# Scores of two query blocks in one visit, and one strip tile for two heads, in a two-layer hybrid attention kernel

## The chip, the cores and the metric

The kernel runs on one core of one Trainium2 chip. The metric is the device time of one execution in microseconds, here the median of three. A core has five engines that run their own streams of instructions side by side and wait for each other through semaphores: TensorE (matmuls and transposes; PE in the profile, PEld for the loads of its stationary operand), VectorE (DVE), ScalarE (ACT), GpSimd (POOL) and SyncE (SP), which here issues most DMAs. TensorE writes to eight banks of PSUM; everything else stands in SBUF.

## The reference

Two identical layers over 1,040 tokens (16 meta tokens ahead of 1,024 drawn ones) with 1,024 features, all in float32. A layer projects x with one matrix and feeds four mixers of eight heads with 64 features each; every mixer's output is multiplied by a SiLU gate, and one output projection, a scaled residual and a layer norm end the layer. Each mixer computes

```
logits = q @ k.T * scale (+ bias or decay), masked by position
probs  = softmax(logits)
out    = probs @ v
```

- A (forgetting attention): dense causal attention, the logits get a decay, cumsum(log f)[t] - cumsum(log f)[s].
- B (latent attention): q and k come from small latents; 32 rotary features are added to the 64 plain ones, so the logits are a sum of two products.
- C (sparse attention): an indexer scores all keys, and each query attends only to its 256 best.
- D (sliding window of 128 keys, with a learned sink in the softmax's sum).

## The kernel before, in words

**Tiles.** The tokens form nine blocks, 0 to 8: block 0 holds the 16 meta tokens, the others 128 tokens each. In A, B and C a query block i of 128 rows attends to 128 i + 16 keys. Keys are cut at multiples of 128 of the packed order, so i tiles of 128 keys are followed by a tile of 16, the "strip". In D a block attends to at most 256 keys in two tiles. The eight heads of a mixer are worked in four pairs, p = 0 to 3, and the two heads of a pair are e = 0 and 1.

**The order of work.** A class `Plan` writes one list of items, and each engine walks through it and issues its part of each item; the list thus sets the order on each engine. A layer runs the branches in the order A, D, B, C, then the output projection and the layer norm. In the first layer (profile times) A runs from 242 to 541 us, D to 797, B to 1080 and C to 1325. `pair` (L366) writes the items of one pair: it goes through the query blocks in `ORDER`, 8 down to 0 (L31), one step each. In the second layer block 0's queries aren't needed, and `empty_step` (L464) takes the step's place. A step of block i writes:

- `qk`: TensorE multiplies q of the block by the keys (L1100; in B a second product with the 32 rotary features, L1111). The scores of both heads go to score banks; a product has up to 512 columns, and `score_products` (L84) cuts it. VectorE adds the bias or mask, takes each row's maximum and writes the scores to a row of `probs` (L1565). `probs` has three rows of different length (`ROW_AT`), used in turn. In A and C, GpSimd prepares the mask of the diagonal first (`tri` L1637, `near` L1652).
- `rec` (of the step before, `normalise` L508): VectorE takes the reciprocal of the sums (L1576, L1577) and GpSimd multiplies the row by it (L1664), once a head.
- `pv` (`values` L493): if the transposes of an odd block were written in the step before, TensorE multiplies the transposed probabilities of the two blocks 2a - 1 and 2a by v (L1136), all into the bank O_BANK. `pv_parts` (L147) lists its products: 2a - 1 tiles with both blocks' 256 query columns, one with 128 columns, and two strips with 16 key rows and 32 columns each. The product is written for e = 0 and 1.
- `tp` for e = 0, then 1, of the block two steps back (`LAG` = 2; `probabilities` L481): TensorE transposes its tiles (L1123) in groups of up to four (`t_groups` L119) into one of two banks of `ps_t`, and ScalarE or VectorE copies each group to the buffer X or Y of `arena` (L1298). Block 8 has nine tiles a head and so three groups. A strip is a transpose like the others, of 16 columns to 16 rows.
- `exp` (L1287): ScalarE's exponential with its sum, one for each head. `gt` (L1585): VectorE multiplies pv's result by the gate. `top`: a number of steps of the top-256 search for branch C (L1328, L1330), set for each step by `TOP_RATE`.
- filler: projections (`tile`, `q_latent`, `k_latent`, `token_block`) for the gate and for the next pair or branch. Each chunk of 340 to 348 columns (L1057, in B L1066) goes through one bank, `P_BANK`, which ScalarE or VectorE empties: the gate by ScalarE (L1255) and then VectorE (L1503), B's rotary chunks by VectorE (L1516 to L1521). The next chunk waits for that.

`flush` (L513) writes what is still pending after the last pair of a branch.

**Waits.** A `pv` waits until all its groups have been copied (`all_left`, L725). A transpose group waits until its bank of `ps_t` has been emptied (`bank_left`, L732). A score product waits until VectorE has read what stood in its banks before. VectorE waits, before it writes a row of `probs`, for the transposes that read the row's last content (`rwaits`).

Most of TensorE's stream in these branches is L1057, L1066, L1100, L1111, L1123 and L1136. A float32 matmul is run as two passes, and the profile counts each pass as an instruction.

## Time and profile before

| | before |
|---|---|
| median of three runs | 3070.66 us (3069.75 to 3072.55) |
| the profiled execution: its time | 3073.53 us |
| its span | 3071.7 us |
| TensorE busy, matmuls | 2929.9 us, 95% |
| VectorE busy | 1656.8 us, 54% |
| ScalarE busy | 1032.8 us, 34% |
| GpSimd busy | 549.7 us, 18% |
| mean granted clock of TensorE over the span | 0.992 |

The span is the time from the profile's first instruction to its last. Times in the rows are microseconds from its start. The granted clock is a share of TensorE's full 2.4 GHz, and 0.50 is its lower level. In a timeline, operations of one form that follow each other are one line: start, duration, engine, line of the code, operation, output and inputs with partitions x elements (for TensorE stationary and moving operand), the number of instructions, and in brackets the idle time before it and what ended it. An end of a matmul is modelled, so its duration is less exact than the start of the next line.

### The profile page before, as it was taken

Reading aid. Unit: us, or ns where it says so; the run is one execution under the profiler, and the core shown is the slowest. Engines: PE = TensorE matmul, PEld = TensorE weight load, DVE = VectorE, ACT = ScalarE, POOL = GpSimd, SP = SyncE. Lnnn points to the kernel's source line nnn. Section 1 sums busy time; section 2 is a strip of 40 time slices with the busy share of each in tenths; the row PEclk is TensorE's granted clock in tenths of the full one; section 3 lists DMA queues with packets and bytes.
Section 4 is the critical chain, followed back from the end, with each engine's and each line's share of the span. In section 5 each row is a group of like instructions: output and inputs, shape, how many; then the busy total and the mean of one; then the engine's idle time right before and its main releaser. Section 6 shows DMA issues by size and latency. Waiting matters only on the chain. (4 is left out here: it accounts for less than half of the span.)

```text
span 3071.7 us, 40390 instructions
## 1 busy us (share of the span) xinstructions
PE 2929.9 (95%) x14262; PEld 1702.8 (55%) x14262; DVE 1656.8 (54%) x4445; ACT 1032.8 (34%) x3121; POOL 549.7 (18%) x946
## 2 busy tenths in 40 slices
PE   7999999998899999999999999999988999999998
PEld 5446666555466666644544466665554666665443
DVE  5338877766777433312233388777667764323222
ACT  3233333333444344410012333333334443444000
POOL 1002222111122133300000022221111111334000
PEclk9999999999999999999999999999999999999999
DMA  5101111101000021042120011111010001210421
GB/s 213 58 14 39 42 43 32 44 27 45 22 17 18 20 79 54 25 143 82 55 87 29 14 39 42 42 32 44 27 51 15 17 18 32 95 32 25 154 82 41
DMA packets 89102, 152.69 MB, mean 50 GB/s; under 512 B 10640, under 2 KB 66592, under 8 KB 86856
## 3 DMA queue, kind: packets, MB, share of 16 engines
q1 hardware_dynamic: 88904, 150.12, 14.9%
q8 instruction: 116, 1.90, 0.3%
q14 instruction: 82, 0.67, 0.1%
HBM read 120.12 MB, written 32.08 MB: 50 GB/s over the span
## 5 line engine op out<-in xcount | busy, mean ns | idle before, releaser
L1057 PE MATMUL ps_s<-xT,w_ring 128*128 128x348 f32 (+4 forms) x3616 | 1127.8, 466 | 11.9 <-DVE arena L1407 4.8
L1057 PEld LDWEIGHTS ps_s<-xT,w_ring 128*128 128x128 f32 x3616 | 674.3, 191 | 407.3 <-issue 113.2
L1664 POOL TENSOR_SCALAR arena<-arena,small 128x1040 f32<-128x1040 f32 (+8 forms) x544 | 353.3, 661 | 1450.6 <-DVE small L1577 1449.3
L1298 ACT ACTIVATE arena<-ps_t 16x32 f32<-16x32 f32 (+4 forms) x1096 | 331.2, 357 | 306.0 <-PE ps_t L1123 298.6
L1287 ACT ACTIVATE arena<-arena,small 128x1040 f32<-128x1040 f32 (+8 forms) x544 | 369.0, 678 | 149.9 <-DVE small L1565 149.7
L1328 DVE MAX8 small<-score 128x8 f32<-128x1040 f32 (+6 forms) x448 | 376.3, 840 | 10.5
L1330 DVE MATCH_REPLACE8 score<-small,score 128x1040 f32<-128x1040 f32 (+6 forms) x448 | 370.0, 826 | 0.0
L1123 PE MATMUL ps_t<-ident,arena 128*128 128x128 f32 (+2 forms) x2400 | 347.3, 277 | 23.0 <-ACT arena L1298 22.0
L1123 PEld LDWEIGHTS ps_t<-ident,arena 128*128 128x128 f32 (+2 forms) x2400 | 252.4, 132 | 149.7 <-issue 78.3
L1136 PE MATMUL ps_o<-arena 128*64 128x256 f32 (+3 forms) x3136 | 282.2, 320 | 19.6 <-ACT arena L1298 18.1
L1100 PE MATMUL ps_s<-feat 64*128 64x272 f32 (+12 forms) x1680 | 296.0, 455 | 3.0 <-ACT squares L1213 3.0
L1151 PE MATMUL ps_s<-arena,feat 128*128 128x512 f32 x640 | 284.8, 597 | 3.5 <-DMA feat<-mixed 3.5
L1136 PEld LDWEIGHTS ps_o<-arena 128*64 128x64 f32 (+1 forms) x3136 | 184.4, 135 | 154.1 <-issue 48.8
L1151 PEld LDWEIGHTS ps_s<-arena,feat 128*128 128x128 f32 x640 | 121.8, 192 | 154.1 <-issue 149.0
L1100 PEld LDWEIGHTS ps_s<-feat 64*128 64x128 f32 (+1 forms) x1680 | 136.6, 183 | 92.3 <-issue 73.2
L1492 DVE SCALAR_TENSOR_TENSOR score<-arena,small,score 128x1040 f32<-128x1040 f32 (+6 forms) x98 | 87.8, 901 | 153.9 <-ACT arena L1272 148.1
L1027 PE MATMUL ps_s<-arena,xT 128*128 128x144 f32 (+1 forms) x512 | 149.7, 446 | 1.6 <-ACT cT L1231 1.6
L1255 ACT ACTIVATE gate<-ps_s 128x348 f32<-128x348 f32 (+3 forms) x96 | 44.0, 458 | 279.7 <-PE ps_s L1057 279.7
L1585 DVE SCALAR_TENSOR_TENSOR mixg<-ps_o,gate 128x256 f32<-128x256 f32 (+1 forms) x144 | 56.3, 391 | 140.1 <-PE ps_o L1136 139.7
L1503 DVE SCALAR_TENSOR_TENSOR gate<-gate,ps_s 128x348 f32<-128x348 f32 (+3 forms) x96 | 48.9, 510 | 145.9 <-ACT gate L1255 145.6
L1027 PE MATMUL ps_s<-vw,xT 128*128 128x512 f32 x256 | 114.0, 598 | 3.0 <-ACT squares L1213 3.0
L1027 PEld LDWEIGHTS ps_s<-arena,xT 128*128 128x128 f32 x512 | 81.2, 194 | 62.0 <-issue 61.9
(161 smaller groups left out, 2229.6 us busy)
## 6 DMA issues: line engine op xcount, KB each, us to landing
w_ring<-in_w_feat SPq DMA_DIRECT2D x78, 512.0 KB, 3.5
mixed<-mixg SPq DMA_DIRECT2D x128, 128.0 KB, 1.7
feat<-mixed SPq DMA_DIRECT2D x16, 1024.0 KB, 6.7
resid<-score SPq DMA_DIRECT2D x16, 512.0 KB, 3.1
score<-resid SPq DMA_DIRECT2D x16, 512.0 KB, 7.6
arena<-in_w_out SPq DMA_DIRECT2D x4, 1536.0 KB, 9.0
cT<-falls SPq DMA_DIRECT2D x8, 520.0 KB, 4.8
feat<-falls SPq DMA_DIRECT2D x8, 520.0 KB, 5.3
```

Source lines behind the costliest of these rows:

```text
L1027: mm = pe.matmul(ps_s[0:M, bank, 0:n], xT[:, k, cols], wv[:, k, :], start=(k == 0), stop=(k == KT - 1))
L1057: mm = pe.matmul(ps_s[:, bank, 0:w], w_ring[:, wt % 2, k, :], xT[:, k, c0:c0 + w], start=(k == 0), stop=(k == KT - 1))
L1100: mm = pe.matmul(score_bank(ch, e)[0:M, 0:ch["w"]], q[r:r + HD, qc], k[r:r + HD, k0 + ch["c0"]:k0 + ch["c0"] + ch["w"]], start=True, stop= ...
L1123: mm = pe.transpose(ps_t[0:w, tg % 2, c * BLK:c * BLK + M], p_row(it, h, k0, w), ident[0:M, 0:M])
L1136: mm = pe.matmul(ps_o[HD * e:HD * e + HD, at:at + w], v_of(br, p, e, kb, rows), arena[0:rows, src:src + w], start=(j == 0), stop=(j == len ...
L1151: mm = pe.matmul(ps_s[0:M, bank, :], mix_in[slot][:, k, 0:M], w_out[k][:, cols], start=(k == 0), stop=(k == 15))
L1287: nc.scalar.activation(p, p, ACT.Exp, scale=-1.0, bias=nm[:, e:e + 1], accum_out=psums[0:M, st % 4, e:e + 1]).then_inc(S["exp_done"], 1)
L1298: a = nc.scalar.activation(dst, src, ACT.Copy)
L1328: dve.max(top8, sc).then_inc(S["top_step"], 1)
L1330: dve.match_replace(sc, top8, sc, TAKEN).then_inc(S["top_step"], 1)
L1492: dve.scalar_tensor_tensor(sc, src, w, sc, ALU.mult, ALU.add).then_inc(S["acc_done"], 1)
L1664: nc.gpsimd.tensor_scalar(p, p, rinv[0:M, st % 4, e:e + 1], 1.0, ALU.mult, ALU.mult).then_inc(S["nrm_done"], 1)
```

## The change

**Rounds.** `rounds_of` lists which query blocks' scores are issued in one `qk` item: in D 8 and 7, 6 and 5, 4 and 3, 2 and 1, and 0 alone; in A, B and C 8 to 4 alone, then 3 and 2, then 1 and 0 (without 0 in the second layer, and `empty_step` follows the last round). One `qk` item has both blocks' score products behind each other on TensorE, in B first all products of 64 features and then all of 32, and both blocks' maxima behind each other on VectorE. Then comes `rec` for the blocks of the round before (in D it comes ahead of `qk`), and `values` once; then, for each of the two blocks, the rest of the step as before, with the lag of two steps. `row_of` gives new places in `probs`, so that two blocks can stand in one row. In B, block 3 (400 keys) is one score product and no longer two, and so is block 2 (272 keys).

**Strips.** GpSimd normalises the 16 strip columns of each head not in place but into a new tile `strips` (128 x 4 x 48, the heads at columns 0 and 32) with an instruction of its own, ahead of the one for the rest. One transpose of 48 columns then serves both heads, in the last group of e = 1. `t_groups` cuts the groups accordingly: block 8 has two groups for e = 0 (before: three), block 4 one (before: two). In the buffers X and Y the strips of a head stand in a 256-column area at the end (`strips_at`), the odd block's from column 96. `pv_parts` has one product fewer: the odd block's strip and the tile beside it are one product of 160 columns with 128 rows, and the even strip has 128 rows too. The rows beyond 16 are zeros, written by GpSimd (`strip_zero`) in A's first pair of each layer; v's rows beyond block 8's 16 are zeroed at the start.

**The wait of pv.** A `pv` waits first for all groups but the last, and ahead of the first product that reads the last group's tiles for that one (`last_from`); where there is a single group it waits for it at its start.

**Size.** The program sets a dynamic DMA scratch size of 8,192.

The core of the diff ("..." where lines are left out):

```diff
+STRIP_ODD = BLK - 32
 P_BANK, O_BANK, T_BANK = 4, 5, 6
+STRIPS = 2
...
+def rounds_of(br):
+    return [[8, 7], [6, 5], [4, 3], [2, 1], [0]] if br == "D" else [[8], [7], [6], [5], [4], [3, 2], [1, 0]]
+def row_of(br, i):
+    if br == "D":
+        n = NB - 1 - i
+        return (0, 256 * n) if n < 4 else (1, 256 * (n - 4)) if n < 6 else (2, 256 * (n - 6))
+    return {3: (2, 0), 2: (2, keys_of(3)), 1: (1, 0), 0: (2, keys_of(3) + keys_of(2))}.get(i, ((NB - 1 - i) % 3, 0))
...
-        products = even(n, 2 if n >= 272 else 1)
+        products = even(n, 2 if i > 3 else 1)
...
-    if br == "D" or i <= 1:
+    if br == "D" or i == 0:
         return [both([kb for kb in range(max(i - 1, 0), i + 1)])] if e else []
-    parts = -(-(i + 1) // 4)
-    size = -(-(i + 1) // parts)
-    return [[(e, kb) for kb in range(c, min(c + size, i + 1))] for c in range(0, i + 1, size)]
+    if i == 1:
+        return [both([0]) + [(STRIPS, i)]] if e else []
+    tiles = [(e, kb) for kb in range(i)] + ([(STRIPS, i)] if e else [])
+    parts = -(-len(tiles) // 4)
+    size = -(-len(tiles) // parts)
+    return [tiles[c:c + size] for c in range(0, len(tiles), size)]
+def tile_at(a, kb):
+    return PT_HEAD[buffer_of(a)] + 256 * (kb - 2 * a)
+def strips_at(a):
+    return PT_HEAD[buffer_of(a)] - 256
...
+    a = (i + 1) // 2
     if kb == i:
-        return 256 * i + 32 if i % 2 else 256 * (i - 1)
-    return kb * 256 + (0 if i % 2 else BLK)
+        return strips_at(a) + (STRIP_ODD if i % 2 else 0)
+    return tile_at(a, kb) + (0 if i % 2 else BLK)
...
-    at = 256 * (2 * a - 1)
-    return ([(kb, BLK, 256 * kb, 256, 0) for kb in range(2 * a - 1)] + [(2 * a - 1, BLK, at + BLK, BLK, BLK),
-            (2 * a - 1, N_META, at + 32, 32, 96), (2 * a, N_META, at, 32, 224)])
+    at = strips_at(a)
+    return ([(kb, BLK, tile_at(a, kb), 256, 0) for kb in range(2 * a - 1)]
+            + [(2 * a - 1, BLK, at + STRIP_ODD, 256 - STRIP_ODD, STRIP_ODD), (2 * a, BLK, at, 32, 224)])
...
+        for blocks in rounds_of(br):
+            if l == DEPTH - 1 and 0 in blocks:
+                blocks = blocks[:-1]
+            steps = [self.step(l, br, p, i, hu) for i in blocks]
+            if br == "D":
+                self.normalise()
+            for s in steps:
+                if br == "A":
+                    self.add("tri", **s)
+                if br == "C":
+                    self.add("near", **s)
+            if steps:
+                self.add("qk", l=l, br=br, p=p, idx=steps[0]["idx"], hu=hu, steps=steps)
+                self.normalise()
+                self.values()
+            self.pending += steps
+            for s in steps:
+                if early and s["idx"] == NB - 1:
+                    early()
+                old = self.pending.pop(0) if len(self.pending) > LAG else None
+                if old and old["i"] == 0:
+                    self.values()
+                self.probabilities(old, 0)
+                self.add("exp", e=0, **s)
+                self.gated()
+                self.add("top", l=l, count=TOP_RATE[br][s["idx"]])
+                work = fill.get(s["idx"], [])
+                for fn in work[:1]:
+                    fn()
+                self.probabilities(old, 1)
+                self.add("exp", e=1, **s)
+                for fn in work[1:]:
+                    fn()
+            self.rec_next += steps
+        if l == DEPTH - 1:
+            self.empty_step(l, br, early, fill.get(NB - 1, []))
...
+        row, at = row_of(br, i)
...
-                self.pv_next = dict(s, need=tg + len(groups))
+                own = [kb for h, kb in groups[-1] if h != STRIPS] if len(groups) > 1 else [0]
+                self.pv_next = dict(s, need=tg + len(groups), last_from=own[0])
...
+            for c, (h, kb) in enumerate(group):
+                if h == STRIPS:
+                    m0, m1 = c * BLK + it["M"] - asks(it["br"], it["i"], kb), c * BLK + it["M"]
+                    for e in range(2):
+                        at = pt_at(it["buf"], e) + pt_col(it["br"], it["i"], kb)
+                        out.append((arena[0:N_META, at:at + m1 - m0], ps_t[32 * e:32 * e + N_META, tg % 2, m0:m1]))
...
+                    for s in it["steps"]:
+                        i, M = s["i"], s["M"]
+                        k0 = keys_of(i) - s["n"]
+                        for ch in s["products"]:
+                            waits(pe, ch["waits"])
...
-                        for j, ch in enumerate(it["products"]):
+                        for j, (s, ch) in enumerate((s, ch) for s in it["steps"] for ch in s["products"]):
+                            i, M = s["i"], s["M"]
                             for e in range(2):
                                 r = HD * (j % 2) + ROPE * e
-                                pe.matmul(score_bank(ch, e)[0:M, 0:ch["w"]], qr[r:r + ROPE, qc],
+                                pe.matmul(score_bank(ch, e)[0:M, 0:ch["w"]], qr[r:r + ROPE, tok0(i):tok0(i) + M],
...
+                            if h == STRIPS:
+                                mm = pe.transpose(ps_t[0:3 * N_META, tg % 2, c * BLK:c * BLK + M],
+                                                  strips[0:M, it["strip"], :], ident[0:M, 0:M])
+                                continue
...
-                    all_left(pe, it["need"])
+                    if it["last_from"]:
+                        all_left(pe, it["need"] - 1)
...
+                        if j == it["last_from"]:
+                            all_left(pe, it["need"])
...
-                    waits(dve, it["rwaits"])
...
+                    for s in it["steps"]:
+                        waits(dve, s["rwaits"])
+                        maxima(s)
...
-            link(nc.gpsimd.memset(fz[:], 0.0))
+            link(nc.gpsimd.memset(v_tok[:, NB - 1, :], 0.0))
+            link(nc.gpsimd.memset(cv_tok[:, NB - 1, :], 0.0))
+            link(nc.gpsimd.memset(strips[:], 0.0))
...
+                    if it["idx"] == 0 and p == 0:
+                        pool.wait_ge(S["pj_full"], vw_used[(l, "TA")])
+                        for buf in "XY":
+                            z = strip_rows(buf)
+                            nc.gpsimd.memset(z, 0.0).then_inc(S["strip_zero"], 1)
...
-                        p = p_row(it, e, 0, it["n"])
-                        nc.gpsimd.tensor_scalar(p, p, rinv[0:M, st % 4, e:e + 1], 1.0, ALU.mult, ALU.mult
-                                                ).then_inc(S["nrm_done"], 1)
+                        inv = rinv[0:M, st % 4, e:e + 1]
+                        if it["br"] == "D" or it["i"] == 0:
+                            p = p_row(it, e, 0, it["n"])
+                            nc.gpsimd.tensor_scalar(p, p, inv, 1.0, ALU.mult, ALU.mult).then_inc(S["nrm_done"], 1)
+                            continue
+                        n = it["n"] - N_META
+                        nc.gpsimd.tensor_scalar(strips[0:M, it["strip"], 2 * N_META * e:2 * N_META * e + N_META],
+                                                p_row(it, e, n, N_META), inv, 1.0, ALU.mult, ALU.mult)
+                        p = p_row(it, e, 0, n)
+                        nc.gpsimd.tensor_scalar(p, p, inv, 1.0, ALU.mult, ALU.mult).then_inc(S["nrm_done"], 1)
...
-    nc = bacc.Bacc("TRN2", target_bir_lowering=False, num_devices=1)
+    nc = bacc.Bacc("TRN2", target_bir_lowering=False, num_devices=1, dynamic_dma_scratch_size=8192)
```

## Rows read from the trace of the kernel before

**Rows 1.** The page: busy time, share of the span and instructions of each engine.
```profile
PE 2929.9 (95%) x14262; PEld 1702.8 (55%) x14262; DVE 1656.8 (54%) x4445; ACT 1032.8 (34%) x3121; POOL 549.7 (18%) x946
```

**Rows 2.** Waits of TensorE: line, releaser: total us, times, longest.
```profile
PE ps_t L1123 <- ACT arena L1298: 22.0, 62, 0.6
PE ps_o L1136 <- ACT arena L1298: 18.1, 24, 1.4
```

**Rows 3.** Groups by shape: line, operation, xcount | busy, mean ns | idle.
```profile
L1123 PE MATMUL ps_t<-ident,arena 128*16 128x128 f32 x400 | 107.4, 273 | 0.0
...
L1664 POOL TENSOR_SCALAR arena<-arena,small 16x16 f32<-16x16 f32 x32 | 8.3, 268 | 81.4 <-DVE small L1577 81.4
```

**Rows 4.** Timeline of TensorE, branch A: start, us, operation xcount.
```profile
441.62 0.82 PE L1123 MATMUL ps_t<-ident,arena 128*128 128x128 f32 x6
442.37 0.73 PE L1100 MATMUL ps_s<-feat 64*128 64x272 f32 x4
443.08 2.95 PE L1136 MATMUL ps_o<-arena 128*64 128x256 f32 x32
445.96 0.76 PE L1123 MATMUL ps_t<-ident,arena 128*128 128x128 f32 x5
446.56 4.85 PE L1057 MATMUL ps_s<-xT,w_ring 128*128 128x348 f32 x16
451.24 0.71 PE L1123 MATMUL ps_t<-ident,arena 128*128 128x128 f32 x5
```

**Rows 5.** The same stretch, TensorE's weight loads (PEld).
```profile
445.61 0.31 PEld L1136 LDWEIGHTS ps_o<-arena 16*64 16x64 f32 x8 [0.17 <-issue]
```

**Rows 6.** Timeline of TensorE in branch D.
```profile
701.68 0.60 PE L1123 MATMUL ps_t<-ident,arena 128*128 128x128 f32 x4
702.21 0.70 PE L1100 MATMUL ps_s<-feat 64*128 64x256 f32 x4
703.03 1.09 PE L1136 MATMUL ps_o<-arena 128*64 128x256 f32 x12
```

**Rows 7.** Timeline of VectorE and TensorE in D, at a gate chunk.
```profile
547.02 0.51 DVE L1503 SCALAR_TENSOR_TENSOR gate<-gate,ps_s 128x344 f32<-128x344 f32 x1
...
548.70 0.56 PE L1057 MATMUL ps_s<-xT,w_ring 128*128 128x348 f32 x1
```

**Rows 8.** Timeline of TensorE in branch B, pair 1.
```profile
915.75 0.95 PE L1100 MATMUL ps_s<-feat 64*128 64x200 f32 x8
...
918.88 1.40 PE L1066 MATMUL ps_s<-cT,vw 128*128 128x344 f32 x4 [0.83 <-DVE feat L1521]
920.11 0.82 PE L1123 MATMUL ps_t<-ident,arena 128*128 128x128 f32 x6
920.86 0.73 PE L1100 MATMUL ps_s<-feat 64*128 64x136 f32 x8
...
921.97 2.95 PE L1136 MATMUL ps_o<-arena 128*64 128x256 f32 x32
...
925.45 1.39 PE L1066 MATMUL ps_s<-cT,vw 128*128 128x348 f32 x4
```

**Rows 9.** Timeline of VectorE in the same stretch.
```profile
924.95 0.33 DVE L1521 COPY feat<-feat 64x344 f32<-64x344 f32 x1
```

**Rows 10.** Timeline of TensorE in branch B, pair 0.
```profile
854.59 2.63 PE L1066 MATMUL ps_s<-cT,vw 128*128 128x344 f32 x4 [2.16 <-DVE feat L1521]
857.02 1.21 PE L1123 MATMUL ps_t<-ident,arena 128*128 128x128 f32 x6
858.16 0.73 PE L1100 MATMUL ps_s<-feat 64*128 64x136 f32 x8
```

**Rows 11.** Windows in B, pair 0: us, busy time by engine, PEclk, DMA share.
```profile
854.40:857.80 3.40, 3.21 (x8) 2.17 (x9) 3.30 (x15) 0.72 (x2) 1.61 (x2) 0.50 0.00 0
```

**Rows 12.** Timeline of TensorE in branch C.
```profile
1139.13 2.08 PE L1136 MATMUL ps_o<-arena 128*64 128x256 f32 x24 [0.97 <-ACT arena L1298]
...
1197.76 0.74 PE L1123 MATMUL ps_t<-ident,arena 128*128 128x128 f32 x5 [0.51 <-ACT arena L1298]
```

More of the change, by code:

```diff
@@ new lines, in pair, with step @@
+        if l == DEPTH - 1:
+            self.empty_step(l, br, early, fill.get(NB - 1, []))
+        return None
+    def step(self, l, br, p, i, hu):
+        st = self.take("st")
+        chunks, products = [], []
+        some = score_products(br, i)
+        for nth, ((c0, w), pieces) in enumerate(some):
+            banks = self.slot_for(len(some), nth, P_BANK)
+            last = self.n["chunk"] + len(pieces) - 1
+            waits = self.banks(banks, ("max_done", 2 * (last + 1)))
+            if O_BANK in banks:
+                waits = latest(waits + [("o_free", self.n["pv"])])
+            products.append(dict(c0=c0, w=w, banks=banks, pieces=len(pieces), waits=waits))
+            chunks += [dict(c0=a, w=b, banks=banks, at=a - c0, g=self.take("chunk"), full=2 * (last + 1))
+                       for a, b in pieces]
+        row, at = row_of(br, i)
+        owner = self.row_owner[row]
+        n = min(keys_of(i), 2 * BLK) if br == "D" else keys_of(i)
+        return dict(l=l, br=br, p=p, i=i, st=st, idx=NB - 1 - i, n=n, M=rows_of(i), chunks=chunks, products=products,
+                    row=row, at=ROW_AT[row] + at, strip=(NB - 1 - i) % 4,
+                    rwaits=latest([owner] if owner else []), a=(i + 1) // 2, hu=hu,
+                    ds=self.take("ds") if br == "D" else None, tri=self.take("tri") if br == "A" else None,
+                    nb=self.take("nb") if br == "C" else None)
@@ L766, in copies @@
             out = []
+            for c, (h, kb) in enumerate(group):
[4 more added lines that the diff above has]
+                        out.append((arena[0:N_META, at:at + m1 - m0], ps_t[32 * e:32 * e + N_META, tg % 2, m0:m1]))
+            if all(h == STRIPS for h, _ in group):
+                return out
             runs, per = copy_runs(it["br"], it["i"], group)
```

133 lines of the change are left out of this document (46 added, 87 removed).

## The prediction

> **What bounds the kernel now.** The page's engine table comes first [rows 1]: TensorE is busy 95% of the span, and with one core that makes every hole and every instruction on TensorE count directly. The waits of TensorE come second [rows 2]: the largest sum is 22.0 us in 62 pieces, transposes that wait until ScalarE has emptied a bank of ps_t, about 0.35 us each. So the end is set by TensorE's own order of work, and a gain must come from fewer or cheaper instructions there; a loss comes where the new order makes it wait for somebody. I then read stretches of its timeline, one in each branch, beside VectorE's.
>
> **The joined strip's transposes.** Six transposes stand between 441.62 and 442.37, four between 701.68 and 702.21 [rows 4, 6]; the difference of two is 0.22 us, so one is 0.11. Each query block i from 1 to 8 of branches A, B and C gives up one: the two heads' 16-column strips become one 48-column tile. That is 8 blocks x 3 branches x 4 pairs x 2 layers = 192 of the 400 narrow ones [rows 3], 192 x 0.11 = 21 us. The same moving columns pass through, so I price the joined one like a single one. The ScalarE copies stay as many.
>
> **The strip's products.** Every matmul of the program stands twice in the trace (two passes of f32). The sixteen-row products are 8 instructions at the end of a sum; their weight loads start at 445.61, behind 0.17 us of idle, and the next transposes start at 445.96 [rows 4, 5], so the strips cost 0.35 us after a change of array shape that costs about 0.09 more (four transposes need 0.44 and the row shows 0.53 before the scores of [rows 6]). In all 0.44. Afterwards the odd strip rides in the tile beside it, 160 columns instead of 128: 16 products of 348 columns run from 446.56 to 451.24, 4.68 us [rows 4], so a column costs 0.84 ns a pass, 32 more in two passes 0.05 us. The even strip stays as two passes, 0.06 each, with 128 rows, and the way out of the shape costs what it did, 0.09. 0.44 - 0.05 - 0.12 - 0.09 = 0.18 us for each of the 4 products a pair with a >= 1: 96 x 0.18 = 17 us.
>
> **Fewer groups.** Block 8 has 9 tiles of head 0 now, in three groups, and the third waits; with 8 it has two. 24 times about 0.3 [rows 2]: 7 us. Starting pv before its last group is copied I cost at nothing: only 24 products wait today, 18.1 us in all [rows 2], and they are those of D and of the small blocks, as blocks 4 and 3 in C at 1139.13 [rows 12], whose last transposes are a single group in the new plan too.
>
> **Joined rounds, on the gain side.** A visit to the scores of one 256-column block lasts 0.82 us (702.21 to 703.03) and its columns are 2 x 256 x 0.84 ns = 0.43 [rows 4, 6]; the rest, and 0.09 on the way in, is paid once for two blocks. 0.82 - 0.43 + 0.09 = 0.48 per joining in D, 4 a pair in either layer, 32 x 0.48 = 15.5 us. In A, B and C the block of 272 columns takes 442.37 to 443.08, 0.71, with 2 x 272 x 0.84 = 0.46 of columns [rows 4]: 0.25 + 0.09, of which 0.06 goes back because pv loses a neighbour of its own array shape in some places; 0.28. There are 24 joinings in layer 0 and 12 in layer 1 (block 0 is gone): 36 x 0.28 = 10, and 2 for the third shape that B enters once instead of twice. Sum 28 us; below, nothing (if a second block pays its loads again), above, 0.6 each (the whole visit but for its columns, and both changes of shape), 68 x 0.6 = 41.
>
> **Joined rounds, what they put in the way.** The second block's scores, and the product pv that used to follow, were also cover: while TensorE did them, VectorE and ScalarE emptied the one projection bank (P_BANK). Now both maxima passes stand on VectorE ahead of that eviction, and the cover stands later.
> - B, pairs 0 to 2, blocks 3 and 2. Before: scores of 3 at 915.75, third rotary chunk at 918.88 (it waited 0.83 for VectorE), scores of 2 at 920.86, pv at 921.97, next chunk at 925.45 [rows 8]. VectorE finished the rotary chunk's copy at 924.95 + 0.33 = 925.28, only 0.17 earlier [rows 9]: this stretch is already VectorE's. In the new order VectorE has block 2's maxima (0.75) ahead of it and 0.27 less for block 3, so the next chunk can start at 925.8; TensorE gets there at 920.11 + 0.65 for six transposes + 0.3 for the bank + 0.44 for four, 921.5, and waits 4.3 us, while the 2.9 us of pv and the scores come after. Pair 0 is alike, pair 2 has narrower top-k steps: 4.3, 4.3 and 3.5, 12 a layer, 24 us. What idleness does to the clock stands in [rows 10, 11]: after 2.16 us without work the granted clock was 0.50 (1.2 instead of 2.4 GHz) for 3.4 us, four chunks took 2.43 us (854.59 to 857.02) against 1.23 (918.88 to 920.11), the transposes behind them 1.14 against 0.75, 1.6 us in all. Six times: 9 us. B: 33 us; bounds 20 (waits of 2.5 and 5 of clock) and 50 (each wait 2 longer, the same clock twice in two places).
> - D. A gate chunk's eviction ended at 547.02 + 0.51 = 547.53, and the next projection began at 548.70 [rows 7]: 1.2 us of slack. A joined round brings 0.8 us more of maxima and 0.7 of sums that wait for the exponential ahead of it on VectorE, and TensorE arrives 0.6 to 1.8 sooner. Three of four pairs then wait 0.5 to 1.8: 12 us over both layers. In layer 0 the product pv of block 1 comes straight behind its transposes, without scores between: 4 x 1.0. The last D steps and the w_tb projections lose 0.6 of cover at about ten boundaries: 6. Together 22; bounds 5 and 35.
> - A. Blocks 5 and 4 now make three groups in a row, 8 x 0.35; the last K chunk is directly ahead of the next pair's scores, 8 x 0.15; in pair 0 VectorE is late, 2 x 0.6. 5 us. The long projection (4.7 us) hides the rest.
> - C has no projection in the last three steps. Waits like the 0.51 at 1197.76 [rows 12] move and grow to about 1.5 in front of blocks 1 and 0, while the 0.97 us that the product of blocks 4 and 3 waits at 1139.13 goes, since block 2's transposes now stand ahead of it. I take 4 us net, bounds 0 and 15.
>
> **Rest.** VectorE's and POOL's new memsets lie in the start, under loads. POOL gets 384 narrow multiplies, by the smallest row 0.27 us [rows 3], ahead of each wide one; POOL is 18% busy and normalises a step before it is asked. For blocks 3 and 2 there is no such step left, but pv of blocks 5 and 6 (2.9 us, [rows 8]) stands between: maxima 0.8, reciprocal 0.2, strip 0.3, wide multiply 0.6, semaphores 0.3, 2.2 us. Nothing, as long as VectorE is on time. No DMA moves to another queue.
>
> **Sum**, against the profiled execution (span 3071.7, own time 3073.5): -21 - 17 - 7 - 28 + 33 + 22 + 5 + 4 = -9, so 3064.5. That execution is 2.9 above the median of the three runs, 3070.7. I forecast 3062 there. A difference under 0.2%, 6 us, can't be told from none.
>
> **Rivals.**
> 1. *The waits are hidden after all.* ScalarE's and VectorE's work is not more, and a wait in one step may only take the place of one in the next. For: the copies before transposes recover quickly. Against: 925.28 against 925.45 in [rows 8, 9], where VectorE has no slack to give. With 15 of the 64 us left (33 + 22 + 5 + 4): 3062 - 49 = 3013.
> 2. *The clock.* Waits of 1 to 2 us in C (6) and D (12) may each bring a stretch at half clock as the 2.16 us of [rows 10, 11] did, 1.6 us each: 29 us, so 3091, slower. It decides once a wait nears 2 us in a stretch that has others beside it. Against: 86 waits of at most 1.4 us for ScalarE's copies stand in the trace [rows 2], and with them the granted clock of the whole span is 0.992 in the mean. The Trainium skill (TensorE: Matmul & The Clock Gate, "HAM oscillation — how this bites in real kernels") says that waits between bursts of matmuls put TensorE back to half clock when they are long, in its example waits of several microseconds for a DMA in each K tile. The trace agrees in kind, with a shorter wait, 2.16 us [rows 10, 11]; by the page's example alone the clock would fall only behind B's waits of 4.3 us and this rival would be empty, by the trace's row it is near, so it keeps its chance.
> 3. *Joining saves half.* If the second block's weight loads stay uncovered or its banks aren't free, the gain of 28 is 14 and the time 3062 + 14 = 3076: no change. For: both blocks' banks must be empty at once. Against: those maxima are a step old.
>
> **How the numbers follow.** Forecast 0.44, own range 3045 to 3064.5 (all of it faster); rival 1 0.13; rival 2 0.22; rival 3 0.21. Faster 0.57, same 0.21, slower 0.22. The range reaches to 7 above rival 1's middle and to rival 2's: 3020 to 3090. Rival 3 at 3076 lies inside what counts as no change.
>
> **What would show it.** Narrow transposes down by 192 and sixteen-row products gone: the first two terms. In B, a wait of L1066's line for VectorE's rotary copy of 3 to 5 us, six times, with the clock at half behind each: the largest term. In D, more than the few gate waits of before. PE busy lower by 60 to 75 us with idle higher by about as much. Wrong would be: no wait over 2 us in B (then rival 1), or half-clock stretches in C and D (rival 2).

## The result and the profile after

The changed kernel takes 3078.68 us in the median of ten runs (3073.24 to 3080.97), the one before 3071.07 in ten: a ratio of 1.0022, 95% interval 1.0012 to 1.0032. The forecast was 3062, faster. The profiled execution took 3078.39 us with a span of 3076.6, against 3073.53 and 3071.7, so 4.9 us more; its mean granted clock was 0.984 instead of 0.992. The page of the kernel after ([rows 1] before):

```profile
PE 2894.3 (94%) x13558; PEld 1696.6 (55%) x13558; DVE 1650.5 (54%) x4381; ACT 1068.3 (35%) x3097; POOL 645.2 (21%) x1336
```

TensorE is busy 36 us less and has 704 instructions fewer, and the span grew all the same: 40 us more went into idle time (the prediction had asked for 60 to 75 us less busy). Its largest waits, by line and releaser, with total us, times and longest ([rows 2] before; L1186 is the transposes' line now, L1203 pv, L1123 B's rotary chunks, L1114 the projections, L1182 the joined strip's transpose; "..." stands for rows left out):

```profile
PE ps_s L1123 <- DVE feat L1614: 26.5, 10, 4.5
PE ps_t L1186 <- ACT arena L1367: 23.9, 59, 0.9
PE ps_o L1203 <- ACT arena L1367: 21.9, 17, 1.6
PE ps_s L1114 <- DVE gate L1596: 12.4, 17, 1.8
...
PE ps_t L1186 <- POOL arena L1755: 9.5, 13, 1.1
```

The first was 6.0 us in four pieces before, the fourth 3.7 us, and the last wasn't there. What was to be removed is removed; the groups by shape (busy us, mean ns) have 192 joined transposes, and products of 160 and 32 columns with 128 rows in the place of the sixteen-row ones ([rows 3] before):

```profile
L1182 PE MATMUL ps_t<-ident,strips 128*48 128x128 f32 x192 | 53.1, 276 | 0.0
...
L1203 PE MATMUL ps_o<-arena 128*64 128x160 f32 x384 | 42.6, 299 | 0.0
...
L1203 PE MATMUL ps_o<-arena 128*64 128x32 f32 x384 | 24.9, 208 | 0.0
```

I cut both executions at the first score product of each branch; C ends with its last pv. The lengths in us, and in the last columns the us in which TensorE was granted its lower clock:

| stage | before | after | difference | half clock before | after |
|---|---|---|---|---|---|
| A, layer 0 / 1 | 298.5 / 295.4 | 291.0 / 290.0 | -7.6 / -5.4 | 0 / 0 | 0 / 0 |
| D | 267.6 / 264.7 | 277.2 / 271.8 | +9.6 / +7.1 | 10.2 / 6.8 | 23.8 / 20.4 |
| B | 271.3 / 267.3 | 276.5 / 277.3 | +5.3 / +10.1 | 3.4 / 3.4 | 13.6 / 20.4 |
| C | 245.8 / 240.5 | 240.8 / 235.2 | -5.0 / -5.3 | 0 / 0 | 0 / 0 |
| start, between and end | 920.6 | 916.8 | -3.8 | 26.1 | 22.3 |

The windows of D and B before (length; busy us by engine with instructions in brackets; then the granted clock and the DMA share):

```profile
540.96:808.61 267.65, 242.12 (x1049) 136.91 (x1048) 188.06 (x506) 105.42 (x379) 44.41 (x108) 0.98 0.11 35
808.61:1079.89 271.28, 264.41 (x1742) 166.34 (x1743) 174.46 (x609) 115.72 (x346) 50.05 (x72) 0.99 0.07 20
2076.22:2340.91 264.69, 237.64 (x1009) 134.77 (x1008) 185.22 (x479) 100.88 (x347) 42.34 (x100) 0.99 0.11 35
2340.91:2608.19 267.28, 260.40 (x1686) 164.40 (x1687) 172.66 (x584) 113.92 (x330) 47.96 (x64) 0.99 0.06 20
```

and after:

```profile
534.46:811.66 277.20, 244.67 (x1062) 141.69 (x1063) 187.43 (x506) 105.23 (x380) 44.78 (x108) 0.96 0.11 35
811.66:1088.21 276.55, 258.42 (x1568) 161.04 (x1568) 172.48 (x577) 122.03 (x340) 65.71 (x134) 0.98 0.06 18
2069.24:2341.06 271.82, 239.13 (x1003) 139.10 (x1003) 184.54 (x479) 100.40 (x348) 42.66 (x100) 0.96 0.11 35
2341.06:2618.40 277.34, 259.26 (x1531) 161.91 (x1532) 170.89 (x552) 120.57 (x324) 63.52 (x128) 0.96 0.06 19
```

A and C gained, D and B lost, and in both the clock is lower by 0.01 to 0.03 of some 270 us. In B the forecast waits are there, one in each of pairs 0 to 2, 4.47, 3.47 and 2.81 us in layer 0 and the same within 0.02 in layer 1, each with a stretch at half clock that begins in it or directly behind it. TensorE in pair 1 after ([rows 8] before):

```profile
924.64 1.40 PE L1123 MATMUL ps_s<-cT,vw 128*128 128x344 f32 x4 [0.59 <-DVE feat L1614]
...
927.51 0.66 PE L1186 MATMUL ps_t<-ident,arena 128*128 128x128 f32 x4 [0.81 <-POOL arena L1755]
931.63 2.66 PE L1123 MATMUL ps_s<-cT,vw 128*128 128x348 f32 x4 [3.47 <-DVE feat L1614]
934.09 0.83 PE L1186 MATMUL ps_t<-ident,arena 128*128 128x128 f32 x4
```

and VectorE beside it ([rows 9] before), from block 3's maxima to the copy that lets the chunk go:

```profile
924.53 0.57 DVE L1451 CUSTOM_DVE_ANT_0 arena<-ps_s,causal 128x400 f32<-128x400 f32 x1
...
925.52 0.44 DVE L1451 CUSTOM_DVE_ANT_0 arena<-ps_s,causal 128x272 f32<-128x272 f32 x1
...
926.97 0.58 DVE L1397 MAX8 small<-score 128x8 f32<-128x400 f32 x1
...
931.15 0.33 DVE L1614 COPY feat<-feat 64x344 f32<-64x344 f32 x1
```

Two blocks' maxima end at 926.3, top-k steps follow, the rotary copy ends at 931.48, and the chunk starts at 931.63 after 3.47 us, behind another 0.81 us for GpSimd that I had not forecast: the reciprocals of block 4 now stand behind both maxima on VectorE, so its normalisation is late. The window behind the wait, with a granted clock of 0.50:

```profile
931.10:934.50 3.40, 2.87 (x6) 1.82 (x7) 3.20 (x9) 0.17 (x1) 0.00 (x0) 0.50 0.00 0
```

### The profile page after: what moved, and what is told of

Read it like the earlier page. It is cut to its first block and busy times, and to the rows that moved or that the text cites. A ratio compares the mean times of both kernels' runs of the same rounds, so it can differ in the third digit from the quotient of the medians.

```text
span 3076.6 us, 39320 instructions
## 1 busy us (share of the span) xinstructions
PE 2894.3 (94%) x13558; PEld 1696.6 (55%) x13558; DVE 1650.5 (54%) x4381; ACT 1068.3 (35%) x3097; POOL 645.2 (21%) x1336
## 3 DMA queue, kind: packets, MB, share of 16 engines
q8 instruction: 111, 1.82, 0.2%
## 5 line engine op out<-in xcount | busy, mean ns | idle before, releaser
L1114 PE MATMUL ps_s<-xT,w_ring 128*128 128x348 f32 (+4 forms) x3616 | 1125.0, 465 | 20.8 <-DVE gate L1596 12.4
L1114 PEld LDWEIGHTS ps_s<-xT,w_ring 128*128 128x128 f32 x3616 | 673.0, 191 | 403.2 <-issue 109.7
L1367 ACT ACTIVATE arena<-ps_t 16x32 f32<-16x32 f32 (+3 forms) x1072 | 373.8, 371 | 256.9 <-PE ps_t L1186 232.2
L1186 PE MATMUL ps_t<-ident,arena 128*128 128x128 f32 (+1 forms) x2016 | 305.2, 279 | 33.8 <-ACT arena L1367 23.9
L1186 PEld LDWEIGHTS ps_t<-ident,arena 128*128 128x128 f32 (+1 forms) x2016 | 231.6, 141 | 161.9 <-issue 84.5
L1752 POOL TENSOR_SCALAR strips<-arena,small 128x16 f32<-128x16 f32 x384 | 108.3, 282 | 935.8 <-DVE small L1652 935.8
L1755 POOL TENSOR_SCALAR arena<-arena,small 128x1024 f32<-128x1024 f32 (+7 forms) x384 | 287.8, 749 | 0.0
L1158 PE MATMUL ps_s<-feat 64*128 64x512 f32 (+10 forms) x1616 | 282.7, 463 | 3.0 <-ACT squares L1280 3.0
L1203 PE MATMUL ps_o<-arena 128*64 128x256 f32 (+5 forms) x2752 | 264.3, 337 | 22.3 <-ACT arena L1367 21.9
L1203 PEld LDWEIGHTS ps_o<-arena 128*64 128x64 f32 (+1 forms) x2752 | 184.2, 137 | 138.9 <-issue 74.7
L1748 POOL TENSOR_SCALAR arena<-arena,small 128x256 f32<-128x256 f32 (+2 forms) x160 | 66.4, 430 | 335.8 <-DVE small L1652 334.9
```

Source lines behind the costliest of these rows:

```text
L1114: mm = pe.matmul(ps_s[:, bank, 0:w], w_ring[:, wt % 2, k, :], xT[:, k, c0:c0 + w], start=(k == 0), stop=(k == KT - 1))
L1158: mm = pe.matmul(score_bank(ch, e)[0:M, 0:ch["w"]], q[r:r + HD, tok0(i):tok0(i) + M], k[r:r + HD, k0 + ch["c0"]:k0 + ch["c0"] + ch["w"]], ...
L1186: mm = pe.transpose(ps_t[0:w, tg % 2, c * BLK:c * BLK + M], p_row(it, h, k0, w), ident[0:M, 0:M])
L1203: mm = pe.matmul(ps_o[HD * e:HD * e + HD, at:at + w], v_of(br, p, e, kb, rows), arena[0:rows, src:src + w], start=(j == 0), stop=(j == len ...
L1367: a = nc.scalar.activation(dst, src, ACT.Copy)
L1752: nc.gpsimd.tensor_scalar(strips[0:M, it["strip"], 2 * N_META * e:2 * N_META * e + N_META], p_row(it, e, n, N_META), inv, 1.0, ALU.mult, A ...
```

## The experiments

All were timed in five rounds against the kernel before on the same chip; a ratio is that of the two with its 95% interval. The kernel before took 3070.7 to 3073.0 us in these sets, so a time of one set against that of another is uncertain by some 2 us, and the ratios are the better measure. Lengths of stages are from one profiled execution of each kernel. An "entry" into pv is the step from the start of TensorE's last instruction before pv to the start of pv's first.

**Strips alone.** The rounds are undone, so that the difference is the joined strip with pv's split wait:

```diff
 def rounds_of(br):
+    return [[i] for i in ORDER]
 def row_of(br, i):
+    return (NB - 1 - i) % 3, 0
-            if br == "D":
+            if br == "D" and len(steps) > 1:
-        products = even(n, 2 if i > 3 else 1)
+        products = even(n, 2 if n >= 272 else 1)
```

> The joined strip and the split wait of pv as in the changed kernel, every query block a round of its own in all four branches. Theory (joined rounds are what costs, by waits in D and B and the half clock behind them; the strip's three terms of 45 us are real): D and B lose what they gained in time, A and C lose 6 us of the joining's gain; 3026 by the terms of the prediction (3071 - 45), 3038 by the changed kernel's stages (3079 - 17 in D - 30 in B + 6). Rival (the strip itself costs: 384 more GpSimd multiplies come ahead of each wide one and the transposes wait for them): near 3065, with waits of the transposes for GpSimd in every branch.

Measured: 3044.66 us, ratio 0.9912 (0.9898 to 0.9925). The strips gain 28 us and not 45. By stage (layer 0 / 1): A -7.9 / -7.0, B -6.4 / -6.3, C -3.0 / -3.1, and D, which has no strips, **+2.7 / +3.4**. The reason in D is seen in one product. Before, a timeline of TensorE and ScalarE:

```profile
633.70 0.60 PE L1123 MATMUL ps_t<-ident,arena 128*128 128x128 f32 x4
...
634.39 0.60 ACT L1298 ACTIVATE arena<-ps_t 128x512 f32<-128x512 f32 x1
...
635.04 1.09 PE L1136 MATMUL ps_o<-arena 128*64 128x256 f32 x12
```

and with strips alone, the same place:

```profile
627.55 0.60 PE L1190 MATMUL ps_t<-ident,arena 128*128 128x128 f32 x4
...
628.24 0.60 ACT L1371 ACTIVATE arena<-ps_t 128x512 f32<-128x512 f32 x1
...
629.10 1.09 PE L1207 MATMUL ps_o<-arena 128*64 128x256 f32 x12 [0.32 <-ACT arena L1371]
```

In both the transposes' copy starts 0.69 us after the transposes; pv starts 0.65 after the copy's start before and 0.86 after it here. Over the 32 entries from scores to pv in D of both layers the entry, from the last score instruction to the first of pv, is 517 ns in the mean before and 697 here, 5.8 us in all, and with the three entries behind transposes 6.3: D's loss. What had changed there is that the wait for the copies stands behind the wait for the output bank, directly ahead of the first matmul. In C, pv waits 1.37 us where it waited 0.97 [rows 12], and around that wait the clock fell (6.8 us at half in either layer, none before):

```profile
1126.69 3.19 PE L1207 MATMUL ps_o<-arena 128*64 128x256 f32 x20 [1.37 <-ACT arena L1371]
```

```profile
1126.00:1129.40 3.40, 2.71 (x14) 1.80 (x16) 0.37 (x5) 0.83 (x3) 2.94 (x10) 0.50 0.01 2
```

The same wait in the next pair has no such stretch (the granted clock from 1186 to 1194 us is 1.00), and the product takes 1.88 us instead of 3.19:

```profile
1188.48 1.88 PE L1207 MATMUL ps_o<-arena 128*64 128x256 f32 x20 [1.37 <-ACT arena L1371]
```

**Rounds alone.** `t_groups`, `pt_col`, `pv_parts` and GpSimd's normalisation are those of before. pv waits for everything in one place, but that place is the late one, behind the wait for the output bank, and now for every pv: the run does not separate the rounds from this wait.

```diff
-                        if it["br"] == "D" or it["i"] == 0:
+                        if True:
-                own = [kb for h, kb in groups[-1] if h != STRIPS] if len(groups) > 1 else [0]
+                own = [0]
```

> Joined rounds as in the changed kernel, without the joined strip and without the split wait of pv: tile groups, buffer layout and products of pv as before. Theory: the kernel before plus what joined rounds cost, 3071 + 41 = 3112 (from 3038) to 3071 + 53 = 3124 (from 3026). Rival (the strip costs, rounds save): 3065 or less.

Measured: 3112.64 us, ratio 1.0132 (1.0118 to 1.0145): joined rounds and the late wait cost 40 us, and the rounds cost 34 to 36 with the strips there (3078.7 - 3044.7, or each against its own kernel before). The prediction's terms for them were -28 + 64 = +36. The stages: A -1.7 / +0.2, D +8.4 / +2.3, B +16.8 / +14.2, C +2.5 / +1.7.

**D single.** `rounds_of` and `row_of` as in the first experiment for D only.

> The changed kernel with D's blocks in rounds of their own (D has no strips, so D is the kernel before in it). Theory: D takes 267.6 and 264.7 us again instead of 277.2 and 271.8, so 17 us less, 3062, and the half-clock stretches behind D's last pair are two again. Rival (D's loss comes from the stage ahead or from GpSimd's order and stays): 3079.

Measured: 3073.32 us (3067.67 to 3077.18), ratio 0.9999 (0.9990 to 1.0008). A miss: 5 us, not 17. D shortened by 5.1 / 3.4 us only; 8 us of its loss stayed, and pv's late wait is there as in the kernel with strips alone, where D loses 6; and in this execution B of layer 0 stood at half clock for 27.2 us instead of 13.6 and took 4.7 us longer, with fewer waits for VectorE's copy there (12.3 us against 13.3).

**B single.** The same for B, with its old two products for blocks 3 and 2.

> The changed kernel with B's blocks in rounds of their own, block 3 and 2 with two products each. Theory: B takes 271.3 and 267.3 us as before less 7.6 us for the strips in each, instead of 276.6 and 277.3, so 30 us less, 3048, with no wait of the rotary chunks over 2.2 us. Rival (B's waits come from GpSimd's extra multiplies or from VectorE's own work, whatever the rounds): above 3070.

Measured: 3050.55 us, ratio 0.9933 (0.9921 to 0.9945): 28 us, as expected. B takes 264.9 and 261.8 us, with half clock for 0 and 6.8 us.

**The wait first, in the changed kernel.**

```diff
-                    if it["last_from"]:
-                        all_left(pe, it["need"] - 1)
+                    all_left(pe, it["need"])
                     if pv:
                         pe.wait_ge(S["o_free"], pv)
...
-                        if j == it["last_from"]:
-                            all_left(pe, it["need"])
```

> The changed kernel, with pv's wait for all its groups standing as in the kernel before: one wait, ahead of those for the output bank. Theory (in the changed kernel the wait for the copies stands last, directly ahead of the first matmul, and the product then starts about 0.2 us later than with the wait first: in the kernel with strips alone the entries from scores to pv in D take 697 ns against 517, and D is 6 us longer, though D has no strips): 0.18 us for each product that waits, some 10 in D, 16 in C and a few in B and A, 4 to 8 us less, 3072; what splitting the wait hides in C (pv there is 2 us a layer longer inside its sum) may give 2 back or take 2. Rival (D's longer entry comes from the copies or from GpSimd, not from where the wait stands): no change, 3079.

Measured: 3071.0 us, ratio 1.0003 (0.9994 to 1.0013), 7.7 us less than the changed kernel, or 5.8 by the two ratios, whose intervals touch at their ends: this alone brings it back to the time before. In D three entries from transposes to pv fall from 1262 to 1059 ns, and three behind the latents' transposes from 1853 to 1650, 0.20 us each. One of the first three, in the changed kernel and here, is shown below. In both, ScalarE's copies start 0.70 us after the transposes that they copy (680.47 to 681.17, and 680.39 to 681.09); pv starts 0.89 us behind the copies' start in the one and 0.69 in the other:

```profile
682.06 1.24 PE L1203 MATMUL ps_o<-arena 128*64 128x256 f32 x12 [0.99 <-ACT arena L1367]
```

```profile
681.78 1.24 PE L1200 MATMUL ps_o<-arena 128*64 128x256 f32 x12 [0.79 <-ACT arena L1364]
```

Summed over all entries into pv of both layers, D gives 3.0 us, C 0.5, and A and B lose 0.7: 2.8 us of direct cost. The other 3 to 5 us came with a higher clock, 0.986 in the mean of the twelve runs against 0.984 in the ten of the changed kernel; at 0.986 the changed kernel took 3073.2 and this one 3070.0 to 3072.1. That fewer stretches at half clock follow from the edit isn't shown. The profiled execution is the slowest of the twelve (3081.86 us), so only single steps are read from it.

**The wait first, strips alone.** The same edit in the kernel with strips alone.

> Strips alone (no joined rounds) with pv's wait as in the kernel before. Theory: D goes back to 267.6 and 264.7 us, 6 us less than with the split wait; with C's part 6 to 10 less than 3044.7, 3037. Rival: D stays at 270.3 and 268.1, 3044.

Measured: 3040.23 us, ratio 0.9904 (0.9891 to 0.9917). D takes 267.3 and 266.6 us (270.3 and 268.1 with the late wait), although layer 1 has 3.4 us more of half clock. A becomes 1.8 us longer in either layer: there the split wait had hidden a copy behind the first products, which I had costed at nothing too. In layer 1 C is longer as well, 239.6 against 237.4 us. The times differ by 4.4 us, the ratios by 2.5, and their intervals overlap; summed over all entries into pv the two kernels are alike (78.4 and 78.2 us, against 68.6 before), D's 5.5 us less standing against A's 3.6 and C's 1.8 more. So with strips alone the edit is worth little, and 10 us of later entries stay.

The pv of blocks 4 and 3 in C shows what makes it later there. ScalarE's last visit ahead of it had two copies before, and here it has three, because both heads' strips come out of the last group; pv waits 1.18 us where it waited 0.97 [rows 12]. Before, then here:

```profile
1138.54 0.54 ACT L1298 ACTIVATE arena<-ps_t 16x32 f32<-16x32 f32 x2
```

```profile
1123.74 0.87 ACT L1368 ACTIVATE arena<-ps_t 16x32 f32<-16x32 f32 x3
...
1124.66 1.88 PE L1204 MATMUL ps_o<-arena 128*64 128x256 f32 x20 [1.18 <-ACT arena L1368]
```

**B's top-k steps moved.**

```diff
-            "B": [4, 4, 5, 5, 5, 5, 5, 4, 1], "C": [0] * 9}
+            "B": [6, 6, 6, 6, 5, 0, 4, 4, 1], "C": [0] * 9}
```

> The changed kernel with B's 38 top-k steps spread over a pair's nine steps as 6, 6, 6, 6, 5, 0, 4, 4, 1 instead of 4, 4, 5, 5, 5, 5, 5, 4, 1: none between block 3's maxima and the rotary eviction behind them. Theory (B's six waits of 3.5 to 4.5 us for the rotary copy are VectorE's queue: two maxima and five top-k steps ahead of the copy): the six waits fall under 1.5 us and the half clock behind them goes, 18 us of waits and 5 to 8 of clock, 3055. Rival (the chunk waits for its data, or the wait only moves to a gate eviction in the first steps): above 3070, with waits for the gate's eviction in B.

Measured: 3049.50 us, ratio 0.9936 (0.9924 to 0.9948), 29 us less with the same rounds. B takes 266.3 and 262.4 us. Its waits of TensorE:

```profile
PE ps_s L1114 <- DVE gate L1596: 12.4, 17, 1.8
...
PE ps_s L1123 <- DVE feat L1614: 11.9, 12, 2.0
```

26.5 us in 10 pieces became 11.9 in 12, the longest 2.0 instead of 4.5, and B's half clock went from 34.0 us to 6.8. So the price was VectorE's queue. Of B's 25 us some 15 are waits; the other 10 I put down to the half clock, 27 us less of it, which gives an estimate of 0.4 us for each. The time is that of the kernel with B single (3050.55), so the shift gives back what joining had cost and no more.

**D's top-k steps moved** too:

```diff
-... "D": [4, 4, 4, 4, 4, 4, 4, 4, 4],
+... "D": [2, 6, 2, 6, 2, 6, 2, 6, 4],
```

> The changed kernel with B's top-k steps moved as in the run before (3049.5) and D's 36 spread as 2, 6, 2, 6, 2, 6, 2, 6, 4 instead of 4 each: two instead of four between a joined round's maxima and the gate eviction behind them. Theory (D's 17 waits for the gate's eviction, 12.4 us, are partly VectorE's queue and partly the plain chain of ScalarE and VectorE that nothing covers any more, 0.46 + 0.51 us and the latencies): the waits fall to about 0.7 each, 4 us less, 3045. Rival (they are all queue): 12 less, 3038. Rival (all latency): 3049, no change.

Measured: 3050.18 us, ratio 0.9930 (0.9918 to 0.9943). No change, the second rival:

```profile
PE ps_s L1114 <- DVE gate L1596: 12.5, 19, 1.2
```

Ten of the 17 waits are D's, 9.5 us; the other seven are A's. Here D has twelve, 9.6 us, and most of them stand although VectorE is idle and waits for the gate itself; the chunk behind still waits 0.76 us, as it did without the shift:

```profile
697.51 0.52 DVE L1596 SCALAR_TENSOR_TENSOR gate<-gate,ps_s 128x348 f32<-128x348 f32 x1 [1.61 <-ACT gate L1322]
...
698.18 4.92 PE L1114 MATMUL ps_s<-xT,w_ring 128*128 128x348 f32 x16 [0.76 <-DVE gate L1596]
```

These are the chain from the chunk's last matmul through ScalarE and VectorE that scores and pv used to cover. Four of D's waits were longer, 0.95 to 1.82 us, behind top-k steps; the shift moved that part to other chunks.

**C alone joined**, strips everywhere, the wait first; then with the split kept only where there is more than one group (the edit shown); then A joined as well. Single rounds are made as in the first experiment, for A, B and D or for B and D:

```diff
-                    if it["last_from"]:
-                        all_left(pe, it["need"] - 1)
+                    all_left(pe, it["need"] - bool(it["last_from"]))
...
-                        if j == it["last_from"]:
+                        if it["last_from"] and j == it["last_from"]:
```

> Strips in A, B and C, joined rounds in C alone, pv's wait as in the kernel before. Theory: what is hidden by nothing in A, D and B stays single, and C keeps its 2 us a layer of joining: 3044.7 - 4 (C) - 6 to 8 (wait) = 3033, the fastest of all. Rival (C's gain needs the split wait): 3038.

> Strips in A, B and C, joined rounds in C alone, and pv's wait split only where the last group isn't the only one, with the whole wait first where it is. Theory: as the kernel with strips, C joined and the undivided wait (3036.2), but A without the 1.8 us a layer that the undivided wait cost there (292.4 against 290.6): 3032 to 3034. Rival (the split itself also costs in D and C): 3036 to 3040.

> The same with joined rounds in A too. By the stages of the changed kernel against those of strips alone, joining in A costs 0.3 and 1.6 us in the two layers: 2 more than the kernel without, 3035. Rival (the prediction's price: 36 joinings of 0.28 and 5 us of waits, in A about 3 less 5): the same answer within 1; a gain of 2 or more would contradict both.

Measured, in this order: 3036.17 us, ratio 0.9890 (0.9876 to 0.9904); **3031.16** us, 0.9865 (0.9850 to 0.9880), the fastest; 3036.24 us, 0.9883 (0.9869 to 0.9896). The page of the second:

```profile
PE 2884.5 (95%) x13686; PEld 1687.7 (56%) x13686; DVE 1654.2 (55%) x4445; ACT 1070.3 (35%) x3097; POOL 644.8 (21%) x1336
```

Its stages against before: A -7.9 / -7.0, D -0.7 / -1.8, B -6.4 / -5.6, C -7.4 / -6.3. The second is 5.0 us faster than the first, of which A is 3.6: the split wait hides a copy there. In the first, C joined is 2.0 and 5.0 us shorter than single in the kernel with strips alone and the same wait, and the way into pv in C falls from 29.3 to 21.7 us over both layers: what the strips' copies cost there, the joining gives back. Joining A costs 0.3 and 2.2 us in A; between the profiled executions (3029.3 and 3037.8 us, further apart than the medians) D adds 4.8, with 6.8 us more of half clock in layer 1 and none more in layer 0, where its code is the same, and why is open.

**Everything joined**, both top-k shifts and this wait:

> The kernel of the run with D's and B's top-k steps moved, all rounds joined, and pv's wait placed as in the fastest variant. Theory: 0.2 us for each product that waits for a single group, 5 us less than that run, 3040, still above the kernel with C alone joined, because D's last pair keeps its 4 us a layer. Rival: the joined rounds catch up, 3033.

Measured: 3042.41 us, ratio 0.9903 (0.9889 to 0.9917), 8 us less than without the edit, where I had expected 5, and 11 above the fastest.

## Why the prediction was wrong

The forecast by stage, from the prediction's own terms (strips 45 / 6 for each branch and layer of A, B and C), beside what the profiled executions show (they differ by 4.9 us, the medians by 7.6):

| stage, both layers | forecast | measured | difference |
|---|---|---|---|
| A | -13.3 | -13.0 | +0.3 |
| D | +6.5 | +16.7 | +10.2 |
| B | +12.7 | +15.3 | +2.6 |
| C | -14.3 | -10.3 | +4.0 |
| the rest | 0 | -3.8 | -3.8 |

**The step that failed** is "Starting pv before its last group is copied I cost at nothing", a cost put at zero for the way into pv. I had read the edit as a wait that comes later or stays. In D it stays, and moves behind another wait, and each product that waits then starts 0.2 us later. Undone in the changed kernel, it takes 7.7 us off (5.8 by the ratios), and 3078.7 less 7.7 is the time before: with it goes the wrong sign. Of these, 2.8 us are seen in the entries, and the rest came with the clock.

That leaves 9 us to the forecast. They are on the strips' side too: strips and split wait gave 28.3 us where I had 45, 16.7 less, and the whole forecast missed by the same 16.7. With strips alone the entries into pv cost 9.8 us more than before, 6.3 of them in D and 3.9 in C, and C stood at half clock for 13.6 us more, 5 us at the estimate of 0.4. "The ScalarE copies stay as many" is true and missed the point: both heads' strip copies now stand in the last group, directly ahead of pv.

**The joined rounds** were right as a net: +36 forecast, +34 to 36 measured, and 31 with the wait first in both kernels (3071.0 - 3040.2). B was right in mechanism and place: six waits of 21.5 us in all where I had 24. That the net fits so well, 28 by the terms and 28.1 by the stages of the changed kernel against strips alone (11.7 + 16.4), is partly luck, since 4.6 us of waits for GpSimd are in it that I had at nothing, and 34 us at half clock where I had six stretches of 3.4. In D the net forecast was +6.5 (22 less 15.5) and the stages give +10.7 (6.9 + 3.8), with 23.8 us more of half clock; at the 0.4 of the top-k experiment that is 10 us, so without it the gain and the waits would about cancel, and the waits were somewhat smaller than the 22 I gave them. In D a single chunk shows what was lost:

```profile
688.23 1.13 PE L1158 MATMUL ps_s<-feat 64*128 64x256 f32 x8
...
694.30 0.60 PE L1186 MATMUL ps_t<-ident,arena 128*128 128x128 f32 x4
695.66 4.92 PE L1114 MATMUL ps_s<-xT,w_ring 128*128 128x348 f32 x16 [0.76 <-DVE gate L1596]
```

Eight score instructions take 688.23 to 689.30, 1.07 us, where one visit of four took 0.82 [rows 6]. That one was among the long ones: D's visits of four took 0.63 to 0.83 us before, 0.70 in the median, so joining two saves 0.34, and with the 0.09 for the way in 0.43 where I had 0.48. Then the chunk behind the next transposes waits 0.76 us for the gate, where there had been scores to do. In the last pair it is worse, as short chunks there wait for ScalarE or VectorE one after the other; three of its rows, and the window behind the last of them:

```profile
779.92 1.10 PE L1077 MATMUL ps_s<-vw,cT 128*128 128x512 f32 x2 [2.15 <-DVE feat L1614]
...
792.43 1.10 PE L1077 MATMUL ps_s<-vw,cT 128*128 128x512 f32 x2 [1.02 <-ACT arena L1271]
794.30 2.36 PE L1123 MATMUL ps_s<-cT,vw 128*128 128x344 f32 x4 [0.78 <-ACT arena L1271]
```

```profile
794.60:804.80 10.20, 8.07 (x22) 3.25 (x22) 5.88 (x19) 2.36 (x7) 1.69 (x4) 0.50 0.01 2
```

This pair takes 68.7 and 67.4 us instead of 64.6 and 63.3. I had given the last steps of D "0.6 of cover at about ten boundaries", 6 us; the last pairs alone lost 8 net of their gain.

**Rival 2, the clock**, was half right: half clock rose from 49.9 to 100.9 us over the span, in D by 27.2 and in B by 27.2, and not in C. It needs no wait of 2.16 us as in [rows 10, 11]: waits of 1.02 and 0.78 us close together in D stood right ahead of such a stretch, and one of 1.37 in C (strips alone) at the start of one. Nor does a wait's length decide: the same 1.37 us a pair later, and three of 1.57 in C of the changed kernel's layer 1, had none. The Trainium skill's example (TensorE: Matmul & The Clock Gate, "HAM oscillation — how this bites in real kernels") has waits of several microseconds; the traces agree that waits bring the lower clock, but not that they must be so long. That the time follows the clock from run to run is seen within the changed kernel's ten runs: the run with a mean clock of 0.986 took 3073.2 us, the five with 0.983 took 3079.0 to 3081.0. **Rival 1** fell (B's waits are not hidden). **Rival 3** fell too, if less clearly: from each score instruction to the next instruction, waits left out, TensorE spends 16.5 us less in the changed kernel and 20.3 less in the one with everything joined and half as much half clock; with 0.09 for each of the 68 ways in, 6 us, that is 23 to 26 where I had 28 and the rival 14.

**The strips' terms** were -21 - 17 - 7 = -45, and 28 came with them. A has -14.9 of its 15, of which the split wait gives 3.6, and B -12.7. C has -6.1: with strips alone its transposes save 4.9 us in layer 0 (33 instructions fewer), as forecast, but pv's entries cost 2.1 more there (12.52 to 14.66 us) and its clock fell. The wait first doesn't mend it (C -3.6 and -0.9); only joined as well does C give -5.6 and -5.9, and -7.4 and -6.3 in the fastest kernel. D's +6.0 is the late wait's: with the wait first D is at -0.3 and +1.9, the latter with 6.8 us more of half clock than before.

**Rest.** "Nothing, as long as VectorE is on time": it wasn't. Thirteen waits for GpSimd's wide multiply, 9.5 us, stand in the changed kernel, none in that with strips alone, and five, 2.4 us, in that with rounds alone:

```profile
PE ps_t L1183 <- POOL arena L1745: 2.4, 5, 0.8
```

So most of them need both: the joined rounds make VectorE's reciprocal late, and the strip multiply (0.28 us at 926.50) then stands ahead of the wide one. Between the layers 4.9 us were gained, in every variant some 2 to 5: before, 6.8 us at half clock stand there at 1349, after none. What makes that stretch come or go stays open.

## What to carry to other kernels

Where several waits stand ahead of one matmul, try the one that ends last in the first place, as it was 0.2 us cheaper here; a wait that is moved is a change even where its condition is the same. Where a copy is made for two heads at once, ask which wait it now stands ahead of. Before work of one engine is grouped, ask what it covered for the single bank that others empty: here the grouping was worth its saving only in C, the branch that has no projection in its last steps (that this is why isn't tested). And look for what stands in the queue of the engine that empties the bank: moving top-k steps by a few places gave back the 29 us that grouping in B had cost.

## What the runs showed of the hardware

- A matmul whose wait stands directly ahead of it, behind a wait that is already met, started 0.2 us later after the release than with the two waits the other way round (1853 against 1650 ns and 1262 against 1059, changed kernel; 697 against 544 in the mean of 32 entries in D, strips alone). The weight load starts late with it (at 629.06 us for the product of 629.10, strips alone). Why isn't shown.
- The granted clock fell to 0.50 around single waits of 1.37 us in C and behind groups of waits of 0.8 to 1.0 us in D; the ones of up to 1.12 us ahead of pv in C before, but also one of 1.37 and three of 1.57, had no such stretch. A us at half clock cost about 0.4 us, an estimate from B with and without the top-k shift.
- The mean granted clock of one program differs between runs (0.983 to 0.986 in the ten of the changed kernel, with 3081 to 3073 us), and an execution can lose in an untouched branch what a variant gained in its own (D single: B of layer 0 +4.7 us, with 13.6 us more at half clock).
